# A hybrid decoder layer on one core: two of the four weight-block sums of the seven-product down projection are made in DRAM by accumulating DMAs

## The chip, the cores and the metric

The kernel runs on 1 core of one Trainium2 chip. The metric is the device time in microseconds (us) of one execution. Five engines work beside each other and meet at semaphores: TensorE (PE in the profile), VectorE (DVE), ScalarE (ACT), GpSimd (POOL) and SyncE (SP). Sixteen DMA engines move the data that SP, ACT and POOL ask for.

## The reference

One layer of a hybrid decoder on 512 tokens and 16 learned meta tokens, model width 2048, all in float32, cut to what matters here:

```
p = rms_norm(h_res) @ w_in                        # 2048 columns in, conv and RWKV heads out
y_conv = short_conv_group(p[:, conv columns])     # width 3, gated
y_rwkv = rwkv7_group(token_shift(p[:, rest]))     # a recurrence over the tokens, 16 heads of 64
h_res += concatenate(y_conv, y_rwkv) @ w_out
h = rms_norm(h_res)
h_res += square(relu(h @ w_up)) @ w_down          # w_up 2048 x 8192, w_down 8192 x 2048
out = rms_norm(h_res)[16:]
```

## The kernel before

**Weights.** Every weight comes in quarters of 128 x 512 float32 (256 KB, in runs of 512 bytes) into a raw buffer. ScalarE rounds it to the upper part (w_hi), VectorE makes the rest (w_lo = raw - w_hi, split_mlp and split), and TensorE multiplies three times (hi by hi, hi by lo, lo by hi). w_hi and w_lo are rings of 8 quarters. SP asks for each quarter as soon as the one that lay in its raw buffer has been split. There are 4 raw buffers (w_raw) until the MLP and 8 in it (w_more as well).

**The recurrence stage.** It goes over 8 pairs of heads, some 91 us each. TensorE's instructions of a pair are one list: 96 steps of the next projection, and between them, at places that the table PACE fixes, the small matmuls of the recurrence (names such as gram0, x16, y0, z2). TensorE takes the list in order, and so do the others. In the middle of a pair the 64 x 64 triangular blocks (NA) are inverted, and their parts are laid out anew by way of DRAM. SP does this in exchange(): at i = 15 NA goes to DRAM (`gram<-NA`, L555), and 80 blocks of 16 x 16 come back onto 80 partitions (`UU<-gram`, L557, 1280 runs of 64 bytes). VectorE inverts them (from L1526 to L1531). At i = 17 they go out (`inverse<-UU`, L561), and at i = 18 they come back as rows (`uni<-inverse`, L564 and L565, and from ACT's queue L1068 and L1069). The step x16 on TensorE (L2001) needs them.

**GpSimd in a pair.** pair() on POOL makes rb_lo (L770) and the two masked copies of NA (nm16 and nm32, L775, four instructions) as soon as VectorE has written NA. Then it issues the DMAs that store the pair's results (L800, L785) and load the next pair's small weights.

**The MLP.** w_up's 8192 columns are taken in 8 groups of 1024. In each of the first 7 groups up() makes 8 tiles of 128 (512 columns of tokens in one matmul), and down() multiplies the group's 1024 rows of w_down by them in a seven-product form (Strassen-Winograd: 2 x 2 blocks of the weights and of the activations, 7 products of half size in place of 8). It takes 8 steps p, each with the products p1, p5, p2, p6, p4, p3, p7 of one tile, 84 matmuls of 256 columns. The last group is taken plainly.

Four of the seven products take a sum of weight blocks, with signs as the form needs them. sum_blocks() makes them on VectorE in three instructions for each p: two sums at once out of a21 and out of a11 and a22 (L1327, 128 x 1024), then a sum with a11 (L1331) and then one with a12 (L1335), both 128 x 512. split_mlp(i) on VectorE calls it before and behind w_lo of p1 and behind w_lo of p5. Splits run 8 quarters ahead of TensorE, so in the last up tile (t = 7) the quarter split is p1 of p = 1, and its sums stand there too, between scale() (L1684, which takes the up tile out of PSUM) and the forms of the activations (L1708 to L1693) that down() waits for.

**The results of down()** are added to the residual in DRAM: one accumulating DMA of 512 KB for each p, issued by POOL (L844, `residual<-delta`).

Of the kernel before, what the change touches and what calls it, by code (L numbers as in the profile page):

```python
# [31 lines left out]
P = 128  # L32
# [81 lines left out]
def at(static, per=0, it=0):  # L114

    return it * per + static
# [95 lines left out]
SUM_STEP = {"p5": 1, "p7": 1, "p6": 2, "p3": 3}  # L212
# [5 lines left out]
L_GROUP = 4 * UT + 4 * HALF_KT  # L218
R_LAST = Q_MLP + R_GROUP * (FFG - 1)
L_LAST = L_GROUP * (FFG - 1)  # L220
T_LAST = T_MLP + UT * FFG
# [10 lines left out]
def hybrid_layer(nc, x, meta, norm_mix_g, w_in, shift_mu, conv_w, decay_w0, decay_w2, iclr_a0, iclr_a2,  # L232
# [4 lines left out]

    res_dram = nc.dram_tensor("residual", [D, SEQ], F32, kind="Internal").ap()
    y_dram = nc.dram_tensor("mixed", [D, SEQ], F32, kind="Internal").ap()
    gram_dram = nc.dram_tensor("gram", [2 * SLOTS * 2, CHUNK], F32, kind="Internal").ap()  # L240
    inv_dram = nc.dram_tensor("inverse", [2 * 2 * SLOTS * 2, CHUNK], F32, kind="Internal").ap()
    as_rows = lambda ap: ap[:, 0:C * C].rearrange("(x a) (r c) -> a r x c", a=2, c=C)
# [127 lines left out]
    w_sum = sb("w_sum", [P, 4, KQ, P], on=post)  # L370
# [55 lines left out]
    sum_made, part_kept, combined = sem("sum_made"), sem("part_kept"), sem("combined")  # L426
    delta_added = [sem("delta_added0"), sem("delta_added1")]
    delta_taken = sem("delta_taken")
    res_back = sem("res_back")
    gained, fin_turned, fin_kept = sem("gained"), sem("fin_turned"), sem("fin_kept")  # L430
    rows_scaled = [sem("rows_scaled_dve"), sem("rows_scaled_act")]
# [52 lines left out]

        return (w_raw if rel % RAW_MLP < RAW else w_more)[:, rel % RAW]

    def raw_pair(p):

        return w_raw if p % 2 == 0 else w_more

    def bank_for(product, p):

        if product in ("p1", "p6", "p7"):
# [16 lines left out]
    wout_q = w_out.rearrange("(a k p) (m n) -> a p k m n", k=KQ, p=P, n=P)  # L510
    wup_q = w_up.rearrange("(a k p) (g m n) -> a p k g m n", k=KQ, p=P, g=FFG, n=P)
    wdn_q = w_down.rearrange("(g a k p) (m n) -> g a p k m n", g=FFG, k=KQ, p=P, n=P)

    RS_CUT = META + 3 * P

# [4 lines left out]
    def _(sp):  # L520
# [83 lines left out]
        def freed_by(rel):  # L604

            shift, i = divmod(rel, L_GROUP)
            if i < R_UP:
                return Q_MLP + R_GROUP * shift + i + 1
            p, b = divmod(i - R_UP, 4)
            return Q_MLP + R_GROUP * shift + R_UP + NP * p + (2, 2, 5, 3)[b]  # L610

        for rel in range(RAW_MLP):
            load_mlp(wup_q[rel % 4, :, :, 0, ORDER[rel // 4], :], rel, Q_MLP - RAW + rel + 1 if rel < RAW else None)
        with sp.Fori(0, FFG - 1) as g:
            for t in range(RAW_MLP // 4, UT):
                for a in range(4):
                    rel = 4 * t + a
                    load_mlp(wup_q[a, :, :, g, ORDER[t], :], rel, freed_by(rel - RAW_MLP), g)
            for p in range(HALF_KT):
                for b, name in enumerate(BLOCKS):  # L620
                    rel = R_UP + 4 * p + b
                    load_mlp(wdn_q[g, int(name[2]) - 1, :, :, p + HALF_KT * (int(name[1]) - 1), :], rel, freed_by(rel - RAW_MLP), g)
# [26 lines left out]
    def _(pool):  # L649
# [99 lines left out]
        def load_g(j):  # L749
            pool.dma_start(g_w[:], gate_g2[0:P, bass.ts(j, P)]).then_inc(g_loaded, 16)  # L750
            for first in range(0, TAIL, GATE_TAIL):
                pool.dma_start(g_w2[first:first + GATE_TAIL, :], gate_g2[P:P + GATE_TAIL, bass.ts(j, P)]).then_inc(g_loaded, 16)

        def pair(j, last=False):
            n = [0]

            def done(name, ins):
                assert POOL_STEPS[n[0]] == name
                n[0] += 1
                ins.then_inc(pool_done, 1)  # L760

            if not last:
                pool.wait_ge(pe_done, step(PE_STEPS, "low", j))
                load_wa(j + 1)

            if last:
                pool.wait_ge(z_done, at(6, 3, j))
                load_y(0, 1)
            pool.wait_ge(act_done, step(ACT_STEPS, "rbh", j))
            done("rbl", nc.gpsimd.tensor_tensor(rb_lo, ld[:, 0:SEQ], rb_hi.bitcast(F32), ALU.subtract))  # L770
            pool.wait_ge(dve_done, step(DVE_STEPS, "gram0", j))
            for i, m in enumerate(LEVELS):
                mask = level_mask[:, i, :].unsqueeze(1).to_broadcast([P, SLOTS, C])
                for h in range(2):
                    ins = nc.gpsimd.tensor_tensor(NM[m][:, h, :, :], NA[:, h, :, 0, :], mask, ALU.mult)  # L775
                done(f"nm{m}", ins)
            if last:
                load_y(2, 3, 4, 5)
            store_conv(j)
            if last:  # L780
                load_y(*range(6, KT - 1))
            else:
                split_squares(j + 1)
                pool.wait_ge(dve_done, step(DVE_STEPS, "y4", j))
                pool.dma_start(y_view[:, bass.ds(j + PAIRS, 1), :], bt[:, PAD + META:TP].unsqueeze(1)).then_inc(y_stored, 16)  # L785
                load_g(j + 1)
# [82 lines left out]
    def _(act):  # L869
# [35 lines left out]
        def split_mlp(i, it=0):  # L905

            shift, j = divmod(i, R_GROUP)
            product = PRODUCTS[(j - R_UP) % NP] if j >= R_UP else None
            if product in SUM_IN:
                act.wait_ge(sum_made, at(3 * ((j - R_UP) // NP) + SUM_STEP[product], 3 * HALF_KT, it))  # L910
                src = w_sum[:, SUM_IN[product]]
            else:
                rel = L_GROUP * shift + (j if product is None else R_UP + 4 * ((j - R_UP) // NP) + BLOCKS.index(BLOCK_IN[product]))
# [343 lines left out]
    def _(dve):  # L1257
# [41 lines left out]
        def split_mlp(i, it=0):  # L1299
# [4 lines left out]
            if product == "p1":  # L1304
                sum_blocks(p, 0, it)
            rel = L_GROUP * shift + (j if product is None else R_UP + 4 * p + BLOCKS.index(BLOCK_IN.get(product, "a11")))
            src = w_sum[:, SUM_IN[product]] if product in SUM_IN else raw_mlp(rel)
            dve.wait_ge(hi_split, at(Q_MLP + i + 1, R_GROUP, it))
            r = (Q_MLP + i) % RING
            V.tensor_tensor(w_lo[:, r], src, w_hi[:, r].bitcast(F32), ALU.subtract).then_inc(lo_split, 1)  # L1310
            if product in ("p1", "p5"):
                sum_blocks(p, 1 if product == "p1" else 2, it)

        def sum_blocks(p, which, it):

            raw = raw_pair(p)

            def loaded(name):
                rel = R_UP + 4 * p + BLOCKS.index(name)
                dve.wait_ge(raw_loaded[rel % RAW_MLP], at(raw_sum(rel), 16 * L_GROUP // RAW_MLP, it))  # L1320

            if which == 0:
                for name in ("a11", "a21", "a22"):
                    loaded(name)
                dve.wait_ge(lo_split, at(Q_MLP + R_UP + NP * p, R_GROUP, it))
                flat = lambda ap: ap.rearrange("p s k n -> p s (k n)")
                V.tensor_tensor(flat(w_sum[:, 0:2]), flat(raw[:, 1:2]).to_broadcast([P, 2, KQ * P]), flat(raw[:, 0:3:2]),  # L1327
                                ALU.add).then_inc(sum_made, 1)
            if which == 1:
                dve.wait_ge(sum_made, at(3 * p + 1, 3 * HALF_KT, it))  # L1330
                V.tensor_tensor(w_sum[:, 2], raw[:, 0], w_sum[:, 1], ALU.add).then_inc(sum_made, 1)  # L1331
            if which == 2:
                loaded("a12")
                dve.wait_ge(sum_made, at(3 * p + 2, 3 * HALF_KT, it))
                V.tensor_tensor(w_sum[:, 3], raw[:, 3], w_sum[:, 2], ALU.add).then_inc(sum_made, 1)  # L1335

        def split_last(i):

# [916 lines left out]
```

## Time and profile before

| | |
|---|---|
| time before, median of 3 runs | 2351.0 us (2350.06 to 2352.89) |
| the profiled execution | 2349.79 us, its span 2348.1 us |
| TensorE busy | 2320.8 us, 99% |
| VectorE busy | 1491.3 us, 64% |
| ScalarE busy | 1019.9 us, 43% |
| GpSimd busy | 299.7 us, 13% |
| DMA | 286.18 MB, 122 GB/s on average |
| chain that ended last | TensorE 91% of the span |

A busy TensorE is the union of its overlapping matmuls, so what lies between 2320.8 and 2348.1 us is all that it stood still. The trace gives the start and the length of every instruction. For a DMA it gives the time from its issue to its landing.

### The profile page before, as it was taken

The numbers are of one execution on the slowest core, as the hardware profiler recorded it, in microseconds if no ns is written. First come the engines' busy times: TensorE is split into PE (matmuls) and PEld (weight loads), VectorE is DVE, ScalarE is ACT, GpSimd is POOL, SyncE is SP. The second block draws the span as 40 slices with busy tenths as digits, with TensorE's granted clock in tenths as the row PEclk, the third lists the DMA queues.
The fourth block names the chain that finished last, engine by engine and source line by source line (L and its number), as shares of the span: only waits on it lengthen the run. The fifth ranks groups of instructions, "written<-read, shape, count | busy, mean of one in ns | idle before, by whom it ended". The sixth has DMA issues, their size and how long they took to land.

```text
span 2348.1 us, 49773 instructions
## 1 busy us (share of the span) xinstructions
PE 2320.8 (99%) x18736; PEld 2087.0 (89%) x18736; DVE 1491.3 (64%) x2338; ACT 1019.9 (43%) x1808; POOL 299.7 (13%) x340
## 2 busy tenths in 40 slices
PE   8999999999999999999999999999999999999998
PEld 8999999999999788889889889889889899899888
DVE  7558668568567654548558468467467476475356
ACT  6534434434344322435435345345345344354336
POOL 5102011011012132101001001001001001001007
PEclk9999999999999999999999999999999999999999
DMA  8244243343343643526527527537447347347434
GB/s 253 72 108 101 68 112 80 93 103 75 98 103 100 181 130 98 179 86 144 145 72 160 138 81 162 131 94 168 110 98 177 99 101 175 94 117 195 120 110 142
DMA packets 513298, 286.18 MB, mean 122 GB/s; under 512 B 84510, under 2 KB 490528, under 8 KB 512672
## 3 DMA queue, kind: packets, MB, share of 16 engines
q1 hardware_dynamic: 478512, 224.19, 34.6%
q0 software_dynamic: 24064, 56.20, 11.8%
q10 hardware_dynamic: 10496, 2.62, 0.6%
q8 instruction: 161, 2.64, 0.5%
q14 instruction: 65, 0.53, 0.1%
HBM read 232.47 MB, written 50.47 MB: 121 GB/s over the span
## 4 chain that ended last, share of the span: by engine, by line
PE 91%; DVE 3%; DMA 3%; issue 1%; ACT 1%; SPq 0%; ACTq 0%; DVEq 0%
PE PD L1894 42%; PE PD L1899 18%; PE PW L2167 5%; PE PW L2168 5%; PE PW L2169 5%; PE PD L2167 2%; PE PD L2168 2%; PE PD L2169 2%; PE PD L2113 1%; PE PD L1923 1%; PE PW L1923 1%; DMA w_raw<-in_w_in 1%; PE PW L1973 1%; DMA gram<-NA 1%; PE PW L2073 1%
## 5 line engine op out<-in xcount | busy, mean ns | idle before, releaser
L1894 PE MATMUL PD<-act_lo,w_hi 128*128 128x512 f32 x1344 | 531.6, 396 | 0.0
L1894 PE MATMUL PD<-act_hi,w_hi 128*128 128x512 f32 x1344 | 529.5, 394 | 0.5 <-issue 0.5
L1894 PE MATMUL PD<-act_hi,w_lo 128*128 128x512 f32 x1344 | 528.5, 393 | 0.0
L2167 PE MATMUL PW<-form_hi,w_hi 128*128 128x256 f32 x1120 | 313.4, 280 | 0.0
L2169 PE MATMUL PW<-form_hi,w_lo 128*128 128x256 f32 x1120 | 312.6, 279 | 0.0
L2168 PE MATMUL PW<-form_lo,w_hi 128*128 128x256 f32 x1120 | 312.6, 279 | 0.0
L1894 PEld LDWEIGHTS PD<-act_hi,w_hi 128*128 128x128 f32 x1344 | 252.4, 188 | 62.7 <-issue 2.0
L1894 PEld LDWEIGHTS PD<-act_hi,w_lo 128*128 128x128 f32 x1344 | 252.9, 188 | 57.5
L1894 PEld LDWEIGHTS PD<-act_lo,w_hi 128*128 128x128 f32 x1344 | 252.1, 188 | 57.8 <-issue 0.2
L1345 DVE TENSOR_TENSOR w_lo<-w_raw,w_hi 128x512 fp32r<-128x512 f32 x268 | 206.7, 794 | 109.0 <-ACT w_hi L930 105.7
L930 ACT CAST w_hi<-w_raw 128x512 fp32r<-128x512 f32 x268 | 160.4, 620 | 252.2 <-DMA w_raw<-in_w_in 113.6
L1899 PE MATMUL PD<-act_hi,w_hi 128*128 128x264 f32 (+1 forms) x1248 | 264.9, 293 | 0.0
L1899 PE MATMUL PD<-act_hi,w_lo 128*128 128x264 f32 (+1 forms) x1248 | 251.3, 283 | 0.0
L1899 PE MATMUL PD<-act_lo,w_hi 128*128 128x264 f32 (+1 forms) x1248 | 251.2, 282 | 0.0
L1310 DVE TENSOR_TENSOR w_lo<-w_raw,w_hi 128x512 fp32r<-128x512 f32 x200 | 137.1, 689 | 125.5 <-ACT w_hi L917 102.6
L2167 PEld LDWEIGHTS PW<-form_hi,w_hi 128*128 128x128 f32 x1120 | 210.5, 188 | 1.7 <-issue 1.4
L1310 DVE TENSOR_TENSOR w_lo<-w_more,w_hi 128x512 fp32r<-128x512 f32 x200 | 137.4, 689 | 116.1 <-ACT w_hi L917 115.4
L2168 PEld LDWEIGHTS PW<-form_lo,w_hi 128*128 128x128 f32 x1120 | 210.5, 188 | 0.3
L2169 PEld LDWEIGHTS PW<-form_hi,w_lo 128*128 128x128 f32 x1120 | 210.5, 188 | 0.0
L844 POOL DMA_DIRECT2D residual<-delta x56 | 66.9, 1195 | 1115.5 <-DVE delta L1732 997.3
L1899 PEld LDWEIGHTS PD<-act_hi,w_hi 128*128 128x128 f32 x1248 | 192.5, 188 | 11.9 <-issue 6.7
L917 ACT CAST w_hi<-w_raw 128x512 fp32r<-128x512 f32 x200 | 123.2, 618 | 180.0 <-PE PD L1894 155.3
(378 smaller groups left out, 4080.7 us busy)
## 6 DMA issues: line engine op xcount, KB each, us to landing
w_raw<-in_w_in SPq DMA_DIRECT2D x200, 256.0 KB, 3.2
w_raw<-in_w_down SPq DMA_DIRECT2D x136, 256.0 KB, 3.0
w_more<-in_w_down SPq DMA_DIRECT2D x136, 256.0 KB, 3.1
w_raw<-in_w_up SPq DMA_DIRECT2D x128, 256.0 KB, 3.1
w_more<-in_w_up SPq DMA_DIRECT2D x128, 256.0 KB, 3.4
residual<-delta POOLq DMA_DIRECT2D x56, 512.0 KB, 5.8
w_raw<-in_w_out SPq DMA_DIRECT2D x64, 256.0 KB, 2.8
residual<-res POOLq DMA_DIRECT2D x4, 2048.0 KB, 10.1
```

The source lines that it names most:

```text
L844: pool.dma_start(res_view[:, p::HALF_KT, :], delta[:, p % 2].rearrange("p (a h) n -> p a (h n)", a=2), accum_op=ALU.add).then_inc(delta_ad ...
L917: nc.scalar.copy(w_hi[:, (Q_MLP + i) % RING], src).then_inc(hi_split, 1)
L930: nc.scalar.copy(w_hi[:, q % RING], w_raw[:, q % RAW]).then_inc(hi_split, 1)
L1310: V.tensor_tensor(w_lo[:, r], src, w_hi[:, r].bitcast(F32), ALU.subtract).then_inc(lo_split, 1)
L1345: V.tensor_tensor(w_lo[:, q % RING], w_raw[:, q % RAW], w_hi[:, q % RING].bitcast(F32), ALU.subtract).then_inc(lo_split, 1)
L1894: ins = M(pd_seq(n)[:, 0:width], w, v[:, k, first:first + width], start=begin, stop=end)
L1899: ins = M(PD[:, 2 * (n % 2) + a, cols], w, v[:, k, start:start + cols.stop - cols.start], start=begin, stop=end)
L1923: ins = M(bank[:, h, cols], w, v[:, k, start:start + cols.stop - cols.start], start=begin, stop=end)
L1973: ins = M(PW[rows_of(c), 2 * h + k // 4, k % 4 * P:(k % 4 + 1) * P], (bt if name == "gram0" else kt)[hs[h], cols], ar[hs[h], :, cols], sta ...
L2167: M(bank_for(product, p), whi, hi, start=begins and k == 0, stop=False, skip_group_check=True)
L2168: M(bank_for(product, p), whi, lo, start=False, stop=False, skip_group_check=True)
L2169: ins = M(bank_for(product, p), wlo, hi, start=False, stop=ends and k == KQ - 1, skip_group_check=True)
```

## The change

Two of the four sums are no longer made on VectorE: s1 = a21 + a22 (p5) and s3 = a11 + a21 (p7). For each group and each sum a DMA now copies the 512 x 1024 block a21 (2 MB, rows of 4 KB) from w_down to a DRAM tensor (copy_block), and a second, accumulating one adds the other block to it (add_block), which waits until the copy has landed. s1 and s3 are then loaded as a fourth and a fifth raw quarter of each p (before: a11, a21, a22, a12; now: a11, s1, a12, a22, s3). VectorE still makes the other two sums, of 128 x 512 each: a11 + s1, and a12 with that.

The sums of groups 0 to 3 are made in the recurrence stage, one for each pair: pair j adds its sum and copies the block of the next. The sums of groups 4 to 6 are made in the MLP, at the head of GpSimd's loop body for groups 0 to 2. All of these DMAs are issued by POOL.

```diff
-BLOCKS = ("a11", "a21", "a22", "a12")
-BLOCK_IN = {"p1": "a11", "p2": "a12", "p4": "a22"}
-SUM_IN = {"p5": 1, "p6": 2, "p3": 3, "p7": 0}
+BLOCKS = ("a11", "s1", "a12", "a22", "s3")
+BLOCK_IN = {"p1": "a11", "p5": "s1", "p2": "a12", "p4": "a22", "p7": "s3"}
+FREED_BY = (3, 3, 4, 5, 7)
+SUM_IN = {"p6": 0, "p3": 1}
+SUMMED_IN_MIX = 4
...
             for p in range(HALF_KT):
                 for b, name in enumerate(BLOCKS):
+                    if name[0] == "s":
+                        if p == 0:
+                            sp.wait_ge(block_summed, at(32, 32, g))
+                            sp.sem_inc(sum_seen, 1)
+                        src = sums_q[name == "s3"][g, :, :, p, :]
...
+        def copy_block(g, column):
+            dst = s3_dram if column else s1_dram
+            pool.dma_start(dst[g], wdn_halves[g, 1, 0]).then_inc(block_copied[column], 16)
+
+        def add_block(g, column, copies, per=0, it=0):
+            pool.wait_ge(block_copied[column], at(16 * copies, 16 * per, it))
+            pool.sem_inc(copy_seen, 1)
+            dst = s3_dram if column else s1_dram
+            pool.dma_start(dst[g], wdn_halves[g, 1 - column, 1 - column], accum_op=ALU.add).then_inc(block_summed, 16)
...
                 done(f"nm{m}", ins)
+            add_block(j // 2, j % 2, j // 2 + 1)
+            if j + 1 < 2 * SUMMED_IN_MIX:
+                copy_block((j + 1) // 2, (j + 1) % 2)
             if last:
                 load_y(2, 3, 4, 5)
             store_conv(j)
...
         split_squares(0)
+        copy_block(0, 0)
         for j in range(PAIRS - 1):
             pair(j)
...
-        with pool.Fori(0, FFG - 1) as g:
+        with pool.Fori(0, FFG - 1 - SUMMED_IN_MIX) as g:
+            copy_block(g + SUMMED_IN_MIX, 0)
+            copy_block(g + SUMMED_IN_MIX, 1)
+            add_block(g + SUMMED_IN_MIX, 0, SUMMED_IN_MIX + 1, 1, g)
+            add_block(g + SUMMED_IN_MIX, 1, SUMMED_IN_MIX + 1, 1, g)
+            add_deltas(g)
+        with pool.Fori(FFG - 1 - SUMMED_IN_MIX, FFG - 1) as g:
+            add_deltas(g)
...
-            if product in ("p1", "p5"):
-                sum_blocks(p, 1 if product == "p1" else 2, it)
+            if product in ("p5", "p2"):
+                sum_blocks(p, 0 if product == "p5" else 1, it)
```

Two places show what moves. The first is GpSimd's order in one pair of the recurrence stage (the second of the 8). Before (L770 is rb_lo, L775 the four masked copies, `mixed` the store of the results):

```order
L770 TENSOR_TENSOR rb_lo<-uni,rb_hi 128x512
L775 TENSOR_TENSOR uni<-NA,level_mask 128x320 x4
L800 DMA mixed<-cx 128x512
L747 TENSOR_TENSOR k_sq_lo<-uni,k_sq_hi 128x528
L785 DMA mixed<-bt 128x512
```

and with the change (the line numbers are those of the changed kernel):

```order
L793 TENSOR_TENSOR rb_lo<-uni,rb_hi 128x512
L798 TENSOR_TENSOR uni<-NA,level_mask 128x320 x4
L775 DMA first_column_sum<-in_w_down 512x1024
L768 DMA second_row_sum<-in_w_down 512x1024
L826 DMA mixed<-cx 128x512
L758 TENSOR_TENSOR k_sq_lo<-uni,k_sq_hi 128x528
L811 DMA mixed<-bt 128x512
```

Two DMAs of 2 MB, the accumulating one first, now stand right behind the masked copies of NA and ahead of the pair's stores.

The second place is VectorE at the last up tile of a group (`form<-PD` is scale(), `form<-form` and `form_lo` are the forms that down() waits for). Before:

```order
L1684 SCALAR_TENSOR_TENSOR form<-PD,rs 128x512
L1320 REGISTER_ALU
L1327 TENSOR_TENSOR w_sum<-w_more 128x1024
L1308 REGISTER_ALU
L1310 TENSOR_TENSOR w_lo<-w_more,w_hi 128x512
L1330 REGISTER_ALU
L1331 TENSOR_TENSOR w_sum<-w_more,w_sum 128x512
L1703 REGISTER_ALU
L1708 SCALAR_TENSOR_TENSOR form<-form 128x256
```

and with the change, behind the same scale() and the same forms:

```order
L1717 TENSOR_TENSOR form_lo<-form,form_hi 128x768
L1343 REGISTER_ALU
L1345 TENSOR_TENSOR w_lo<-w_more,w_hi 128x512
L1355 TENSOR_TENSOR w_sum<-w_more 128x512
L1343 REGISTER_ALU
L1345 TENSOR_TENSOR w_lo<-w_more,w_hi 128x512
L1358 REGISTER_ALU
L1359 TENSOR_TENSOR w_sum<-w_more,w_sum 128x512
```

The sums have moved from ahead of the forms to behind them, and the one of 128 x 1024 is gone.

## Rows read from the trace of the kernel before

**Rows 1.** The page, part 1: busy time, share of the span, instructions

```profile
PE 2320.8 (99%) x18736; PEld 2087.0 (89%) x18736; DVE 1491.3 (64%) x2338; ACT 1019.9 (43%) x1808; POOL 299.7 (13%) x340
```

**Rows 2.** Waits of TensorE, 1000 to 2150 us: total, times, longest

```profile
PE PD L2167 <- DVE form_lo L1693: 6.1, 7, 0.9
```

**Rows 3.** Up, then down: us; busy of PE, PEld, DVE, ACT, POOL; clock; DMA share; GB/s

```profile
1136.00:1225.00 89.00, 89.00 (x387) 72.19 (x386) 41.94 (x67) 30.86 (x49) 1.20 (x1) 1.00 0.36 100
1225.00:1304.00 79.00, 78.11 (x666) 77.67 (x665) 64.86 (x105) 45.60 (x91) 8.35 (x7) 1.00 0.68 153
```

**Rows 4.** Timeline of VectorE behind an up stage: start, length, instruction

```profile
1225.32 0.69 DVE L1684 SCALAR_TENSOR_TENSOR form<-PD,rs 128x512 f32<-128x512 f32 x1 [1.43 <-PE PD L1894]
1225.93 1.22 DVE L1327 TENSOR_TENSOR w_sum<-w_more 128x1024 f32<-128x1024 f32 x1
...
1228.27 0.42 DVE L1708 SCALAR_TENSOR_TENSOR form<-form 128x256 f32<-128x256 f32 x1
...
1229.27 0.68 DVE L1693 TENSOR_TENSOR form_lo<-form,form_hi 128x512 fp32r<-128x512 f32 x1
```

**Rows 5.** Timeline of TensorE at the same place; idle before it in brackets

```profile
1230.01 0.38 PE L2167 MATMUL PD<-form_hi,w_hi 128*128 128x256 f32 x1 [0.88 <-DVE form_lo L1693]
```

**Rows 6.** Tile w_sum, one of two buffers: duration ns min/median/max, first and last

```profile
L1327 DVE TENSOR_TENSOR w_sum<-w_raw x28: 1215/1215/1220, 1038.5 to 2122.0; 128x1024 f32<-128x1024 f32 x28
L1331 DVE TENSOR_TENSOR w_sum<-w_raw,w_sum x28: 682/685/687, 1040.3 to 2123.8; 128x512 f32<-128x512 f32 x28
```

**Rows 7.** Timeline of SP's DMA queue in the third pair

```profile
303.48 0.34 SPq L557 DMA_DIRECT2D UU<-gram  x1
...
313.02 1.02 SPq L561 DMA_DIRECT2D inverse<-UU  x2
...
316.50 0.60 SPq L564 DMA_DIRECT2D uni<-inverse  x1
```

**Rows 8.** Timeline of GpSimd in the third pair

```profile
297.20 4.86 POOL L775 TENSOR_TENSOR uni<-NA,level_mask 128x320 f32<-128x320 f32 x4 [0.54 <-DVE NA L1474]
```

**Rows 9.** Timelines of VectorE and of TensorE in the third pair

```profile
306.33 0.07 DVE L1526 MEMSET UU<- 80x16 f32 x1 [1.60 <-DMA UU<-gram]
...
323.42 0.69 PE L2001 MATMUL PW<-uni 64*64 64x64 f32 x32
```

**Rows 10.** DMA issues, 295 to 345 us: KB each, us to landing

```profile
UU<-gram SPq DMA_DIRECT2D x1, 80.0 KB, 2.7
...
uni<-inverse SPq DMA_DIRECT2D x1, 80.0 KB, 5.6
```

**Rows 11.** Waits of TensorE, 180 to 750 us (six pairs)

```profile
PE PW L2001 <- DMA uni<-inverse: 0.4, 1, 0.4
```

**Rows 12.** DMA, 968 to 982 us: packets, MB, share; then issues

```profile
q0 software_dynamic: 994, 4.01, 77.3%
q1 hardware_dynamic: 918, 0.46, 12.2%
...
residual<-res POOLq DMA_DIRECT2D x2, 2048.0 KB, 11.3
w_more<-in_w_up SPq DMA_DIRECT2D x4, 256.0 KB, 11.1
```

**Rows 13.** DMA, 1068 to 1077 us, one accumulating DMA: packets, MB, share

```profile
q0 software_dynamic: 272, 0.52, 40.2%
```

**Rows 14.** The last pair: GpSimd's timeline, then the chain, and its DMA issues

```profile
756.22 1.11 POOL L796 DMA_DIRECT2D yin<-mixed  x2
...
757.64 4.57 DMA UU<-gram
...
yin<-mixed POOLq DMA_DIRECT2D x4, 256.0 KB, 4.0
```

**Rows 15.** Windows with two 2 MB DMAs under way, and behind the last matmul

```profile
968.00:982.00 14.00, 14.00 (x59) 10.72 (x58) 9.06 (x12) 5.93 (x11) 1.82 (x2) 1.00 0.90 319
...
2340.00:2348.00 8.00, 0.00 (x0) 0.00 (x0) 1.58 (x3) 2.31 (x3) 0.00 (x0) 0.53 0.66 262
```

More of the change, by code:

```diff
@@ L217 @@
 R_GROUP = R_UP + NP * HALF_KT
-L_GROUP = 4 * UT + 4 * HALF_KT
+L_GROUP = 4 * UT + NB * HALF_KT
 R_LAST = Q_MLP + R_GROUP * (FFG - 1)
@@ L239, in hybrid_layer @@
     y_dram = nc.dram_tensor("mixed", [D, SEQ], F32, kind="Internal").ap()
+    s1_dram = nc.dram_tensor("second_row_sum", [FFG, SEQ, DH], F32, kind="Internal").ap()
+    s3_dram = nc.dram_tensor("first_column_sum", [FFG, SEQ, DH], F32, kind="Internal").ap()
     gram_dram = nc.dram_tensor("gram", [2 * SLOTS * 2, CHUNK], F32, kind="Internal").ap()
@@ L428, in hybrid_layer @@
     delta_taken = sem("delta_taken")
+    block_copied = [sem("block_copied_s1"), sem("block_copied_s3")]
+    block_summed, copy_seen, sum_seen = sem("block_summed"), sem("copy_seen"), sem("sum_seen")
     res_back = sem("res_back")
@@ L512, in hybrid_layer @@
     wdn_q = w_down.rearrange("(g a k p) (m n) -> g a p k m n", g=FFG, k=KQ, p=P, n=P)
+    wdn_halves = w_down.rearrange("(g y r) (x n) -> g x y r n", g=FFG, y=2, x=2)
+    sums_q = [d.rearrange("g (k p) (m n) -> g p k m n", p=P, n=P) for d in (s1_dram, s3_dram)]
     RS_CUT = META + 3 * P
@@ L608, in freed_by @@
                 return Q_MLP + R_GROUP * shift + i + 1
[L609 to L610 removed]
+            p, b = divmod(i - R_UP, NB)
+            return Q_MLP + R_GROUP * shift + R_UP + NP * p + FREED_BY[b]
         for rel in range(RAW_MLP):
@@ L620, in _ @@
                 for b, name in enumerate(BLOCKS):
-                    rel = R_UP + 4 * p + b
-                    load_mlp(wdn_q[g, int(name[2]) - 1, :, :, p + HALF_KT * (int(name[1]) - 1), :], rel, freed_by(rel - RAW_MLP), g)
+                    rel = R_UP + NB * p + b
+                    if name[0] == "s":
[3 more added lines that the diff above has]
+                        src = sums_q[name == "s3"][g, :, :, p, :]
+                    else:
+                        src = wdn_q[g, int(name[2]) - 1, :, :, p + HALF_KT * (int(name[1]) - 1), :]
+                    load_mlp(src, rel, freed_by(rel - RAW_MLP), g)
             for t in range(RAW_MLP // 4):
@@ L909, in split_mlp @@
             if product in SUM_IN:
-                act.wait_ge(sum_made, at(3 * ((j - R_UP) // NP) + SUM_STEP[product], 3 * HALF_KT, it))
+                act.wait_ge(sum_made, at(2 * ((j - R_UP) // NP) + SUM_IN[product] + 1, 2 * HALF_KT, it))
                 src = w_sum[:, SUM_IN[product]]
             else:
-                rel = L_GROUP * shift + (j if product is None else R_UP + 4 * ((j - R_UP) // NP) + BLOCKS.index(BLOCK_IN[product]))
+                rel = L_GROUP * shift + (j if product is None else R_UP + NB * ((j - R_UP) // NP) + BLOCKS.index(BLOCK_IN[product]))
                 act.wait_ge(raw_loaded[rel % RAW_MLP], at(raw_sum(rel), 16 * L_GROUP // RAW_MLP, it))
@@ L1303, in split_mlp @@
             p = (j - R_UP) // NP
-            if product == "p1":
-                sum_blocks(p, 0, it)
-            rel = L_GROUP * shift + (j if product is None else R_UP + 4 * p + BLOCKS.index(BLOCK_IN.get(product, "a11")))
+            rel = L_GROUP * shift + (j if product is None else R_UP + NB * p + BLOCKS.index(BLOCK_IN.get(product, "a11")))
             src = w_sum[:, SUM_IN[product]] if product in SUM_IN else raw_mlp(rel)
@@ L1310, in split_mlp @@
             V.tensor_tensor(w_lo[:, r], src, w_hi[:, r].bitcast(F32), ALU.subtract).then_inc(lo_split, 1)
-            if product in ("p1", "p5"):
-                sum_blocks(p, 1 if product == "p1" else 2, it)
+            if product in ("p5", "p2"):
+                sum_blocks(p, 0 if product == "p5" else 1, it)
         def sum_blocks(p, which, it):
[L1316 to L1320, printed above, removed]
+            at_ = R_UP + NB * p
             if which == 0:
-                for name in ("a11", "a21", "a22"):
-                    loaded(name)
+                dve.wait_ge(hi_split, at(Q_MLP + R_UP + NP * p + 2, R_GROUP, it))
                 dve.wait_ge(lo_split, at(Q_MLP + R_UP + NP * p, R_GROUP, it))
[L1326 to L1335, printed above, removed]
+                V.tensor_tensor(w_sum[:, 0], raw_mlp(at_), raw_mlp(at_ + 1), ALU.add).then_inc(sum_made, 1)
+            else:
+                dve.wait_ge(hi_split, at(Q_MLP + R_UP + NP * p + 3, R_GROUP, it))
+                dve.wait_ge(sum_made, at(2 * p + 1, 2 * HALF_KT, it))
+                V.tensor_tensor(w_sum[:, 1], raw_mlp(at_ + 2), w_sum[:, 0], ALU.add).then_inc(sum_made, 1)
         def split_last(i):
```

7 lines of the change are left out of this document (3 added, 4 removed).

## The prediction

> **What bounds the kernel now.** I read the busy shares of the page first. TensorE works 2320.8 of 2348.1 us [rows 1], so everything that a change can give back by relieving another engine lies in the 27 us in which TensorE stands. VectorE's 1491 us are no bound by themselves.
>
> The waits of TensorE come next. In the whole MLP but its last group there is one kind that counts, 6.1 us in 7 waits of up to 0.9 us, for form_lo [rows 2]. That is once per group, at the turn from up to down. The windows of one group agree: 89.00 of 89 us busy in the up stage, 78.11 of 79 in the down stage [rows 3]. VectorE is busy for 64.9 of those 79 us, below its limit.
>
> Then the recurrence stage, where TensorE's list is gapless too: in six pairs it waits for the inverse's blocks once, for 0.4 us [rows 11]. That is a chain that is met just in time, not one that is short. I followed it in the third pair, on the timelines. The read back of NA is issued at 303.48 and lands 2.7 us later [rows 7, 10]. VectorE starts on it at 306.33 [rows 9]. The parts go out at 313.02, are asked back at 316.50, and the later of the two reads lands 5.6 us after its issue, at about 316.50 + 0.60 + 5.6 = 322.7 [rows 7, 10]. TensorE takes x16 at 323.42 [rows 9]. So this chain of three trips through DRAM has 0.7 us to spare. While VectorE waits for the read at L1526, its later splits and its copies out of PSUM stand behind it, so TensorE would first stop at a tile that needs a bank, and then at x16; the end of it is the same.
>
> **The change, part by part.**
>
> *VectorE, removed.* Per p the 1.215 us sum becomes one of 0.685 us (a11 + s1), the two others become one: 1.215 + 0.685 + 0.685 - 2 x 0.685 = 1.2 us less [rows 6], the third taken as long as the second. Over 56 p that is 68 us of VectorE. TensorE waits for VectorE in one place only, so most of it is worth nothing. The place is the turn: between scale() at 1225.32 and the first form at 1228.27 stand the sum of 1.22 us, one split, and the second sum [rows 4]. Both sums leave. The instructions overlap a little, so about 1.7 us go: form_lo would be ready that much before its end at 1229.95, where TensorE waited 0.88 us for it [rows 4, 5]. The wait goes entirely, **-6.1 us** in 7 groups. What would be late next is ScalarE's rounding of the same forms; it starts from the same instructions that move up, so I count on no new wait. Below, this gain is 0 if the wait only changes its name; it can't be above 6.1.
>
> *Loads in the down stage.* Five quarters per p in place of four: 8 x 256 KB = 2.1 MB more in 79 us. The queue's price at 512-byte runs is 12.2% of 14 us for 0.46 MB [rows 12], 3.7 us per MB, so 8 us more: the DMA share goes from 0.68 to about 0.78 [rows 3]. A raw buffer is freed at least 8 quarters, some 11 us, before its next content is split; even beside 4 MB of other traffic a load took 11.1 [rows 12]. Cost 0; the cover is the ring of 8 split quarters.
>
> *The sums of groups 4 to 6.* Each time 4 DMAs of 2 MB at the head of an up stage. Their price: 77.3% of 14 us moved 4.01 MB [rows 12], so 5.7 us for a copy of 2.1 MB. The accumulating DMA took 40.2% of 9 us for 0.52 MB [rows 13], 3.6 us; by its bytes that is 14.6 us for 2.1 MB, by its packets (272 against 528) 7.0 us. Together 25 to 41 us beside an up stage that uses 0.36 of the DMA engines for 89 us [rows 3]. Where 4 MB of such traffic ran before, four weight quarters took 11.1 us to land [rows 12], and TensorE was still busy for all 14 us [rows 15]: 16 quarters lie ahead of it there. I take 0, with 5 us a group as the other end.
>
> *The sums of groups 0 to 3, in the recurrence stage.* This is the term that decides. POOL is done with the masked copies at 297.20 + 4.86 = 302.06 [rows 8] and issues the accumulating DMA there, then the copy; its wait for the copy before is long satisfied, and nothing else of its own is due soon behind them. The read `UU<-gram` is issued at 303.48, 1.4 us later, on the same 16 engines. What happens to it? Two places of the trace tell.
> - In the last pair two reads of 256 KB each are issued by POOL at 756.22, again 1.4 us before the read back of NA at 757.64, which then takes 4.57 us in place of 2.7 [rows 14, 10]. At 2.7 us per MB the two are 1.4 us of work: the read waited for all of it, and a bit.
> - Beside the two 2 MB stores, the queue of the weights got 0.46 MB through against 4.01 MB, in 918 packets against 994 [rows 12]. It went packet by packet, so a queue of small packets loses by their size. The read back of NA is in 1280 packets of 64 bytes; the add and the copy together are 1024 of 4 KB. Turn by turn, it would be done no earlier than both of them.
>
> So behind the add alone the read lands 14.6 us late, and with the copy 14.6 + 5.7 = 20.3. Less 0.7 us to spare, 13.9 and 19.6 us a pair. The copy is issued only when the add's descriptors are written, about when the read arrives, so I take **15 us** in each of 7 pairs, and 14 in the last, which has no copy: 7 x 15 + 14 = **+119 us**. At the low end the add costs 7.0 us by its packets and is alone ahead: 8 x 6.3 = +50. At the high end both are ahead at full price: 7 x 19.6 + 14 = +151. TensorE takes its list in order, so no matmul fills the hole.
>
> The Trainium skill, "DMA: Bandwidth & Descriptors", section "Queues, rings and completion order", says that each DMA engine goes round its queues packet by packet. The 918 against 994 packets agree. By this rule taken strictly, the sum would be the high end, +151 - 6 = +145 us, in place of +113.
>
> *TensorE's clock.* It is granted 1.00, the 2.4 GHz level, in every working window. Behind the last matmul it stood still, and 8 us of that are at 0.53, which is 1.2 GHz for nearly all of it [rows 15]. Holes of 14 us may bring this down, and the first matmuls behind each may run at half speed. No row shows how it rises again; I put 0 in the sum and 2 us a pair, +16, at the high end.
> The Trainium skill, "TensorE: Matmul & The Clock Gate", Part 1, says that an idle window drops the clock to half and some microseconds of work restore it; by it some 2 us a pair would be added, an estimate.
>
> **Sum.** -6.1 + 119 = +113 us on the profiled execution's 2349.8 us: 2463. The median of the runs is 1.2 us above that execution: **2464 us**.
>
> **The rivals.**
> - *The DRAM traffic is hidden.* The engines are half idle in the recurrence stage, and if small reads overtook the large packets nothing would be late: 2351 - 6 = **2345 us**, faster by 0.26%. For it: no wait of TensorE came from the stores of rows 12. Against it: those had 16 quarters of cover, this chain has 0.7 us. It decides at a delay of under 0.8 us a pair (6.1 / 8).
> - *The first read escapes, the second trip is caught.* If the add's first packets come after the 303.48 read, it lands on time. The parts' way out at 313.02 [rows 7] then waits for the end of add and copy, near 303.5 + 1 + 20.3 = 325, in place of landing by 316.5: 8.5 us, less 0.7. 7 x 7.8 = 55, little in the last pair, less 6: **2400 us**.
> - *Dearer still.* Both ends of these DMAs are in DRAM, which no row shows. If that doubles the add, or the up stages of three groups run dry of weights, +190 us or more: **above 2540 us**.
>
> **How the numbers follow.** A measurement of this kernel can tell about 0.2%, 5 us. Chances: the forecast with its ends, 2397 to 2530, 0.59; the second trip caught (from 2375 to 2397 when the add is cheap), 0.20; hidden, 0.10; the loss within a microsecond a pair, so that gain and loss cancel, 0.04; dearer, 0.07. The range is 2375 to 2530: outside are hidden, cancelled and dearer. Low end: the second-trip case with the add at 7.0 us; high end: 151 + 16 + 15 - 6 = 176, 2527. Faster 0.10, same 0.04, slower 0.86.
>
> **What would show it.** In the changed kernel's waits: TensorE's row for form_lo gone, and new rows in the recurrence stage, at L2001's successor for the inverse or at the start of a tile for VectorE's copy out of PSUM, about 15 us a pair. SP's read of the 64-byte blocks should take 16 to 23 us to land in place of 2.7, the add some 15 and the copy 6 us more than their fixed part. VectorE's busy time falls by 68 us; each MLP group loses 0.9 us. If the read back of NA still lands in 3 us, the step that fails is the one on who waits at the DMA engines, and the time is one of the first two rivals'.

## The result, and the profile after

The change makes the kernel slower: 2507.6 us (median of 4 runs, 2497.9 to 2512.6) against 2350.5 us, ratio 1.066, interval 1.064 to 1.069. The forecast was 2464 us, in a range of 2375 to 2530. The profiled execution took 2497.9 us, its span is 2496.4 us.

The page of the kernel after: busy shares and instructions, then the chain that ended last by engine.

```profile
PE 2332.9 (93%) x18736; PEld 2098.3 (84%) x18736; DVE 1431.4 (57%) x2282; ACT 1013.5 (41%) x1808; POOL 324.4 (13%) x368
...
PE 81%; DMA 10%; DVE 6%; issue 1%; ACT 1%; SPq 0%; POOL 0%; ACTq 0%; DVEq 0%; POOLq 0%
```

VectorE lost 60 us of busy time, where 68 were foreseen. The lengths of its instructions, added up, fall by 70 us, but neighbours overlap a little, and busy time counts that once. TensorE now stands for 2496.4 - 2332.9 = 163.5 us, where it was 27 [rows 1], and it is busy for 12 us more with the same 18736 instructions. Its waits say where (total, times, longest):

```profile
PE PD L1923 <- DVE cu L1605: 118.7, 7, 17.1
PE PD L2137 <- DVE cu L1605: 12.1, 1, 12.1
PE PD L1918 <- DVE form L1708: 8.7, 1, 8.7
PE PD L1918 <- issue: 6.2, 3, 3.1
```

Seven waits of 17 us and one of 12 are the eight pairs of the recurrence stage. The row for form_lo [rows 2] is gone. The two others are in up stages of the MLP. VectorE's copy out of PSUM (`cu`, L1605) is named, but VectorE itself was held. Its own waits have this row:

```profile
DVE UU L1550 <- DMA UU<-gram: 160.4, 8, 20.9
```

In the third pair the chain in order of time (start, length) and the DMA issues of 335 to 400 us (KB each, us to landing) show the read back of NA. Before, it took 2.7 us [rows 10]:

```profile
341.62 21.41 DMA UU<-gram
```

```profile
second_row_sum<-in_w_down POOLq DMA_DIRECT2D x1, 2048.0 KB, 15.4
first_column_sum<-in_w_down POOLq DMA_DIRECT2D x1, 2048.0 KB, 22.1
...
inverse<-UU SPq DMA_DIRECT2D x2, 80.0 KB, 2.8
UU<-gram SPq DMA_DIRECT2D x1, 80.0 KB, 21.4
```

The read ends with the copy. The second trip, `inverse<-UU`, is as fast as it was, as the traffic is over by then.

GpSimd's timeline has the two DMAs where the order of instructions put them. The add is issued 1.6 us and the copy 0.9 us ahead of the read at 341.62, so both are there before it:

```profile
340.00 1.11 POOL L775 DMA_DIRECT2D second_row_sum<-in_w_down  x1
340.71 1.03 POOL L768 DMA_DIRECT2D first_column_sum<-in_w_down  x1
```

Windows of the same pair (length; busy of PE, PEld, DVE, ACT, POOL; granted clock; DMA share; GB/s):

```profile
355.00:360.00 5.00, 0.00 (x0) 0.00 (x0) 0.00 (x0) 0.00 (x0) 0.00 (x0) 0.75 0.99 309
360.00:365.00 5.00, 0.00 (x0) 0.00 (x0) 1.60 (x9) 1.08 (x2) 0.00 (x0) 0.50 0.40 115
...
370.00:372.00 2.00, 1.01 (x4) 1.01 (x5) 1.93 (x4) 0.00 (x0) 0.00 (x0) 0.50 0.64 63
372.00:374.00 2.00, 2.00 (x12) 2.00 (x11) 1.96 (x4) 0.00 (x0) 0.00 (x0) 0.50 0.73 150
374.00:376.00 2.00, 2.00 (x16) 2.00 (x16) 0.84 (x2) 0.57 (x1) 0.00 (x0) 0.86 0.52 120
376.00:378.00 2.00, 2.00 (x19) 2.00 (x18) 1.29 (x2) 0.05 (x1) 0.33 (x1) 1.00 1.33 241
```

While TensorE stands, its clock falls to 0.50, the 1.2 GHz level. It starts again at 371 us, still at that level, and 1.00 is back 3.6 us later (1.01 and 2.00 us of the windows above, and 0.56 us of the one at 0.86). Half of that is lost, some 1.8 us in this pair. In seven pairs that is about the 12 us of added busy time.

In the MLP, SP's timeline for group 0 shows the up stage running dry. Beside the two copies and the two adds, the issue alone of four weight quarters took 24 us:

```profile
1130.83 24.26 SPq L606 DMA_DIRECT2D w_more<-in_w_up  x4
1155.34 16.26 SPq L606 DMA_DIRECT2D w_raw<-in_w_up  x4
```

### The profile page after: what moved, and what is told of

It is laid out like the page before. It is cut to its first block, busy times and chain, and to the rows that moved or that the text cites. A ratio compares the mean times of both kernels' runs of the same rounds, so it can differ in the third digit from the quotient of the medians.

```text
span 2496.4 us, 49726 instructions
## 1 busy us (share of the span) xinstructions
PE 2332.9 (93%) x18736; PEld 2098.3 (84%) x18736; DVE 1431.4 (57%) x2282; ACT 1013.5 (41%) x1808; POOL 324.4 (13%) x368
## 4 chain that ended last, share of the span: by engine, by line
PE 81%; DMA 10%; DVE 6%; issue 1%; ACT 1%; SPq 0%; POOL 0%; ACTq 0%; DVEq 0%; POOLq 0%
PE PD L1918 35%; PE PD L1923 15%; DMA UU<-gram 7%; PE PW L2192 5%; PE PW L2193 5%; PE PW L2191 5%; PE PD L2192 2%; PE PD L2193 2%; PE PD L2191 2%; DMA w_more<-in_w_up 2%; PE PD L2137 1%; DMA gram<-NA 1%; DVE w_lo L1369 1%; PE PD L1947 1%; PE PW L1947 1%
## 5 line engine op out<-in xcount | busy, mean ns | idle before, releaser
L1923 PE MATMUL PD<-act_hi,w_hi 128*128 128x264 f32 (+1 forms) x1248 | 270.7, 299 | 118.7 <-DVE cu L1605 118.7
L967 ACT CAST w_hi<-w_raw 128x512 fp32r<-128x512 f32 x268 | 161.4, 620 | 394.3 <-DMA w_raw<-in_w_in 228.8
L1345 DVE TENSOR_TENSOR w_lo<-w_raw,w_hi 128x512 fp32r<-128x512 f32 x256 | 175.1, 689 | 181.0 <-ACT w_hi L954 141.1
L1345 DVE TENSOR_TENSOR w_lo<-w_more,w_hi 128x512 fp32r<-128x512 f32 x256 | 175.7, 690 | 166.2 <-ACT w_hi L954 160.9
L1369 DVE TENSOR_TENSOR w_lo<-w_raw,w_hi 128x512 fp32r<-128x512 f32 x268 | 207.2, 796 | 106.8 <-ACT w_hi L967 103.7
L954 ACT CAST w_hi<-w_raw 128x512 fp32r<-128x512 f32 x256 | 157.1, 617 | 217.5 <-PE PD L1918 142.2
L954 ACT CAST w_hi<-w_more 128x512 fp32r<-128x512 f32 x256 | 157.1, 618 | 204.7 <-PE PD L1918 147.4
```

The costliest lines, as they stand in the source:

```text
L967: nc.scalar.copy(w_hi[:, q % RING], w_raw[:, q % RAW]).then_inc(hi_split, 1)
L1369: V.tensor_tensor(w_lo[:, q % RING], w_raw[:, q % RAW], w_hi[:, q % RING].bitcast(F32), ALU.subtract).then_inc(lo_split, 1)
L1923: ins = M(PD[:, 2 * (n % 2) + a, cols], w, v[:, k, start:start + cols.stop - cols.start], start=begin, stop=end)
```

## The experiments

**Each part alone.** First the VectorE side without any DRAM traffic. In the changed kernel the calls of copy_block and add_block are left out, with SP's wait for the sums, and the two added quarters come from another block of w_down, so the down product's results are those of wrong blocks.

```diff
-                        src = sums_q[name == "s3"][g, :, :, p, :]
+                        src = wdn_q[g, 0, :, :, p + HALF_KT, :]
...
-            add_block(j // 2, j % 2, j // 2 + 1)
-            if j + 1 < 2 * SUMMED_IN_MIX:
-                copy_block((j + 1) // 2, (j + 1) % 2)
```

> The changed kernel without its sums in DRAM: no copying and no accumulating DMA is issued, and in place of s1 and s3 SP loads the block a21 straight from w_down, five quarters per p as in the changed kernel; the results of the down product are those of wrong blocks. What stays is the VectorE side of the change and the fifth load. Theory A (all of the loss comes from the DMAs that POOL issues, and the wait for form_lo at the turn from up to down is gone with the sums that stood ahead of it): 2350.5 - 6 = 2344 to 2345 us, and no row for form_lo among TensorE's waits. Theory B (the fifth load or the new order of VectorE costs something itself): above 2350 us, with a new wait of TensorE in the down stages.

Measured: 2339.6 us, ratio 0.995 (0.994 to 0.997), 11.3 us faster. A holds in its mechanism, with nearly twice the size; there is no row for form_lo among TensorE's waits.

The kernel before with the recurrence stage's traffic alone (its results unused):

```diff
                 done(f"nm{m}", ins)
+            add_block(j // 2, j % 2, j // 2 + 1)
+            if j + 1 < 2 * SUMMED_IN_MIX:
+                copy_block((j + 1) // 2, (j + 1) % 2)
```

> The kernel before, with the copying and accumulating DMAs of the recurrence stage added (the first copy and one add and one copy behind the masked blocks in each pair, all as in the changed kernel) and their results unused; VectorE makes its four sums as before. Theory A (the loss is the read of the 16 x 16 blocks that stands behind this traffic): 17 us of standing per pair and 2 us for the lower clock behind it, 7 x 19 + 14 = 147 us, so 2498 us, with the read landing after 21 us. Theory B (the recurrence stage and the MLP share the loss, as the fifth load and the traffic of the MLP cost too): under 2460 us.

Measured: 2494.3 us, 1.061 (1.060 to 1.063), +143.4 us against the kernel before in the same runs (2350.9). A holds. Its waits are those of the changed kernel, with the old row for form_lo back:

```profile
PE PD L1922 <- DVE cu L1604: 118.5, 7, 17.4
PE PD L2136 <- DVE cu L1604: 12.2, 1, 12.2
PE PD L2190 <- DVE form_lo L1716: 6.1, 7, 0.9
```

And with the traffic of the MLP alone:

```diff
+        with pool.Fori(0, FFG - 1 - SUMMED_IN_MIX) as g:
+            copy_block(g + SUMMED_IN_MIX, 0)
+            copy_block(g + SUMMED_IN_MIX, 1)
+            add_block(g + SUMMED_IN_MIX, 0, 1, 1, g)
+            add_block(g + SUMMED_IN_MIX, 1, 1, 1, g)
+            add_deltas(g)
```

> The kernel before, with only the six sums of the MLP added (two copies and two accumulating DMAs at the head of GpSimd's loop body for groups 0 to 2), results unused. Theory A (the up stages run dry of weights for a few us, as the trace of the changed kernel shows 8.7 and 6 us of waits in its first two groups): 2350.5 + 15 = 2362 to 2370 us. Theory B, that of the prediction (hidden by the 16 quarters that lie ahead of TensorE): within 1 us of the kernel before.

Measured: 2369.5 us, 1.008 (1.006 to 1.010), +18.6 us. A holds, and the zero of the prediction falls. 15 of the 18.6 us are in new waits of TensorE:

```profile
PE PD L1923 <- issue: 7.6, 2, 4.2
PE PD L1923 <- DVE form L1713: 7.3, 1, 7.3
```

The three parts add up to -11.3 + 143.4 + 18.6 = +150.7, against +157.1 for the whole.

**The gain without the change.** In the kernel before, only VectorE's order at the last up tile is changed:

```diff
                 scale(t)
-                split_mlp(e + RING, g)
+                if t < UT - 1:
+                    split_mlp(e + RING, g)
                 dve.wait_ge(u_sq, at(t + 1, UT, g))
...
                     low(t, 4, 7, 3)
+                if t == UT - 1:
+                    split_mlp(e + RING, g)
```

> The kernel before, with nothing moved to DRAM: at the last up tile of a group VectorE makes the forms of the activations first, and then the split and the sums of weight blocks that stood ahead of them. Theory A (what the change gains is only that these 1.7 us leave that place): the same gain as with VectorE's sums taken away, 2344 to 2345 us. Theory B (the gain, where there is one, needs VectorE's lower load): no change, or slower as the splits of the first products come 2 us later.

Measured: 2340.3 us, 0.996 (0.994 to 0.997), 10.6 us faster, the same as the VectorE side of the change (2339.6). The 60 us of VectorE's work were worth nothing beyond the place of two sums. Why 10.6 and not 6.1? TensorE's timeline of before, the matmul ahead of the wait that [rows 5] shows:

```profile
1228.86 0.28 PE L2169 MATMUL PD<-form_hi,w_lo 128*128 128x256 f32 x1
```

The next one starts at 1230.01, 1.15 us later, where 0.12 is usual in this stretch: 1.03 us are lost, and the wait counts 0.88, since a matmul's modelled end lies behind the next one's start. The matmuls right behind the wait come late as well. The sixth of them is this one:

```profile
1230.97 0.28 PE L2169 MATMUL PW<-form_hi,w_lo 128*128 128x256 f32 x1
```

The five steps to it took 0.96 us in place of 0.59. Why they did, the trace does not show; with the new order both losses are gone. Together they are 1.4 us. The up tile that the chain names behind each down stage gives the period of a group, before and then with the new order:

```profile
1643.42 11.15 PE PD L1894 x48
1812.50 11.15 PE PD L1894 x48
```

```profile
1637.82 11.15 PE PD L1897 x48
1805.53 11.15 PE PD L1897 x48
```

169.1 and 167.7 us, the same 1.4 us a group; from the first group to the last the two traces part by 9.3 us.

**Who waits at the DMA engines.** Three variants of the traffic beside the read. First, the changed kernel with the read in 80 runs of 1 KB:

```diff
-sp.dma_start(UU[0:NBLK, 0, :].rearrange("b (s t) -> b s t", t=BASE), gram_blocks[:, 0])
+sp.dma_start(UU[0:NBLK, 0, :], gram_dram[0:2 * SLOTS * 2, 0:C // BASE * BASE * BASE].rearrange("m (b e) -> m b e", e=BASE * BASE))
```

> The changed kernel, where the read back of NA onto 80 partitions takes the same 80 KB as 80 runs of 1 KB in place of 1280 of 64 bytes (other elements than it needs, so the layer's result is wrong). Theory A (the DMA engines go round the queues packet by packet: the read has 80 packets on each engine against 32 of the add and 32 of the copy, so it can't end before both; with 5 packets on each it needs 5 turns): it lands within 3 to 6 us. The second trip, issued some 10 us after the read's issue, is then the one that is caught until the traffic ends 20 us after that issue: about 8 us of standing per pair in place of 17, and 2440 us in all. Theory B (first come, first served: the read stands behind all that was queued before it, whatever its packets are): it still takes some 20 us to land, and the time stays near 2500 us.

Measured: 2462.0 us, 1.047. The chain of its third pair:

```profile
330.30 9.29 DMA UU<-gram
...
346.59 10.21 DMA inverse<-UU
```

B falls: the same 80 KB, issued at the same place, land in 9.3 us in place of 21.4. The second trip is now the one caught, as A said. A's number (2440) was too low. TensorE stands for 10 us a pair in place of 8 (35.4 us in seven waits for the inverse's blocks and 35.1 in seven for `cu`), and there are now two holes in each pair, with the granted clock at 0.50 behind both:

```profile
348.00:351.00 3.00, 3.00 (x16) 3.00 (x15) 2.76 (x5) 0.29 (x1) 0.00 (x0) 0.50 0.86 206
363.50:368.00 4.50, 4.46 (x64) 4.14 (x68) 1.99 (x3) 1.24 (x2) 0.00 (x0) 0.50 0.94 258
```

TensorE's busy time is 2355.3 us, 22 us more than in the changed kernel, whose standing is longer but in one piece.

Why the read took 9.3 us and not 3 to 6, the packets say. First DMA queues of this run from the read's issue at 330.3 to 334.9 us (q0 is POOL's queue, q1 SP's; packets, MB, share), then the changed kernel's from 346.6 to 351.6 and from 351.6 to 356.6:

```profile
q0 software_dynamic: 156, 0.64, 93.2%
```

```profile
q0 software_dynamic: 244, 1.00, 103.0%
q1 hardware_dynamic: 242, 0.02, 7.6%
...
q0 software_dynamic: 374, 1.47, 96.5%
q1 hardware_dynamic: 375, 0.02, 7.1%
```

Once the read has its turn, packet goes for packet: 242 beside 244, 375 beside 374, whether they hold 64 bytes or 4 KB. Ahead of that, no packet of SP's queue is moved for 4.6 us, while 156 of POOL's are, 10 for each engine. That the engines had taken these already is a guess; the trace does not show where they stood.

Second, the changed kernel with the copy issued at the end of the pair:

```diff
-            if j + 1 < 2 * SUMMED_IN_MIX:
-                copy_block((j + 1) // 2, (j + 1) % 2)
...
                 load_g(j + 1)
+                copy_block((j + 1) // 2, (j + 1) % 2)
```

> The changed kernel, where only the accumulating DMA stays behind the masked blocks and the copy of the next block is issued at the end of the pair, behind its last store and small loads. Theory A (turn by turn, the read has to wait for each of the 4 KB packets that are there, 32 per engine of the add at 0.33 us and 32 of the copy at 0.2 us): the read lands 12 to 13 us after its issue in place of 21, the standing falls from 17 to 8 or 9 us a pair, and the time to about 2507 - 7 x 8.5 = 2447 us. Theory B (the add alone is what it waited for, the copy runs behind the read): no change, near 2505 us.

Measured: 2454.4 us, 1.045, 53 us less than the changed kernel; A (2447) holds, B falls. The read landed after 14.5 us, and the seven waits fell from 118.7 to 67.8 us:

```profile
PE PD L1922 <- DVE cu L1604: 67.8, 7, 10.0
PE PD L2136 <- DVE cu L1604: 12.1, 1, 12.1
```

The read waited for the copy too, although that is issued behind the add. The last pair, which never had a copy, is unchanged.

Third, half of the traffic: dram_sums_beside_recurrence with `[0:256]` behind both operands of its copies and adds.

> dram_sums_beside_recurrence (2494.3 us) with the first 256 of the 512 rows in each of its copies and adds: half the traffic, at the same places. Theory A (the read of the 16 x 16 blocks, with 80 packets per engine, outlasts the 16 and 16 packets of add and copy too, so the standing is the length of the traffic less what the chain has to spare): the read lands after 11 to 12 us, 8 us of standing a pair and 1 to 2 us of low clock, 2350.5 + 7 x 9 + 5 = 2419 us. Theory B (a fixed cost of a large transfer beside the read): above 2460 us.

Measured: 2422.8 us, 1.031, against 2419 expected. DMA issues of 320 to 330 us, and TensorE's waits:

```profile
UU<-gram SPq DMA_DIRECT2D x1, 80.0 KB, 12.9
```

```profile
PE PD L1922 <- DVE cu L1604: 51.9, 7, 8.3
PE PD L2136 <- DVE cu L1604: 7.0, 1, 7.0
```

Half the bytes, half the loss (72 of 143 us): the large fixed cost of B is not there.

**Other places for the traffic.** Add and copy behind the store of the convolution's result, when the inverse is back:

```diff
             store_conv(j)
+            add_block(j // 2, j % 2, j // 2 + 1)
+            if j + 1 < 2 * SUMMED_IN_MIX:
+                copy_block((j + 1) // 2, (j + 1) % 2)
```

> The changed kernel, with the add and the copy of each pair issued behind the store of the convolution's result, when the inverse's blocks are back, in place of ahead of the read. Theory A (the loss is the place: nothing small and urgent runs in the 20 us behind this point, only weight quarters): the read lands in 3 us again, and what stays is the up stages' 19 us less the 11 us gained on VectorE, plus up to 5 us a pair if the weight quarters, at one packet in turn with one of 4 KB, come late: 2360 to 2395 us. Theory B (any 20 us of such traffic in a pair costs about as much, as the weights then come late): above 2440 us.

Measured: 2399.0 us, 1.021 (1.019 to 1.023). The read lands in 2.5 us again. But 2399 - 2350.5 - 18.6 + 11.3 = 41 us are still lost in the recurrence stage, above what A allowed (2395) and far below B. The waits are spread over many steps now, most of them for ScalarE or with no releaser shown:

```profile
PE PW L2061 <- ACT uni L1110: 12.1, 1, 12.1
PE PW L2093 <- issue: 8.1, 6, 2.4
```

In the third pair the four weight quarters issued beside add and copy took 17.2 us to land (median), and ScalarE, which rounds them in order, comes late to its steps of the recurrence. The longest wait, 12.1 us, has another cause. It is in the last pair, where the chain runs over a load of stored results that POOL issued behind the add:

```profile
802.51 17.27 DMA yin<-mixed
```

So part of what is lost is again a small, urgent load behind large packets.

The same, with the MLP's six sums one to a group, in groups 0 to 5:

```diff
+        for i in range(2 * (FFG - 1 - SUMMED_IN_MIX)):
+            n, column = SUMMED_IN_MIX + i // 2, i % 2
+            copy_block(n, column)
+            add_block(n, column, n + 1)
+            add_deltas(i)
+        add_deltas(FFG - 2)
```

> As sums_behind_the_inverse, and the six sums of the MLP are made one per group in groups 0 to 5, in place of two per group in groups 0 to 2: a copy and an add of 2 MB at the head of each up stage. Theory A (16 quarters of cover in the up stage hold for 17 us of such traffic, not for 34): the 19 us of the MLP go, so 15 to 20 us less than sums_behind_the_inverse. Theory B (the same bytes cost the same wherever they are): the same time as sums_behind_the_inverse.

Measured: 2394.1 us (2386.9 to 2402.3), against 2399.0 (2392.2 to 2400.2): no difference that these runs can tell. In the MLP the run before had three waits, 14.3 us together. Now there are five small ones, and one more of 3.9 us:

```profile
PE PD L1916 <- DVE w_lo L1343: 12.5, 5, 3.4
```

So A fails here. Half as much at a time runs the up stage dry twice as often: one copy and one add are already too much in a row.

**Small pieces.** Each DMA of 2 MB is cut into four of 512 KB, issued one at a time (but for the first copy and the sum of the last pair), none near the inverse's trips. In the MLP one sum is made per group, in groups 0 to 5:

```diff
+                for n_, name in enumerate(("pq", "gh", "y0", "z3", "z5", "z7", "y", "var")):
+                    pool.wait_ge(pe_done, step(PE_STEPS, name, j))
+                    pool.sem_inc(copy_seen, 1)
+                    if n_ % 2 == 0:
+                        add_piece(j // 2, j % 2, n_ // 2)
+                    else:
+                        copy_piece((j + 1) // 2, (j + 1) % 2, n_ // 2)
...
+            for t in range(8):
+                pool.wait_ge(quarter_used, Q_MLP + R_GROUP * i + 4 * (t + 1) - 3)
+                pool.sem_inc(copy_seen, 1)
+                (copy_piece if t < 4 else add_piece)(n, column, t % 4)
```

> The changed kernel, all of its sums made, but in pieces of 512 KB that POOL issues one at a time: in each pair of the recurrence stage four pieces of the add and four of the next copy, each behind one of TensorE's steps pq, gh, y0, z3, z5, z7, y and var (none near the three trips of the inverse), the last sum in the stage of the output projection, and in the MLP one sum per group, one piece at each up tile. Theory A (what costs is only that 16 to 34 us of large packets stand together, ahead of something that is due sooner; the bytes alone cost nothing): as with no traffic at all, 2339.6 us measured, so 2338 to 2345 us. Theory B (the bytes cost wherever they are, as the pair of experiments behind the inverse suggests): 2370 us or more.

Measured over 11 runs: 2348.7 us, 1.000 (0.999 to 1.001): the same bytes, and the time of the kernel before. That is 9 us above the 2339.6 us that A named, and A's range ended at 2345; it is far below B's 2370. The windows of this kernel, the recurrence stage (to 830 us) and the MLP's first seven groups, then its waits for weights:

```profile
0.00:830.00 830.00, 818.44 (x9710) 760.46 (x9711) 568.07 (x895) 361.24 (x599) 182.98 (x258) 1.00 0.60 148
...
1000.00:2150.00 1150.00, 1142.90 (x7264) 1028.94 (x7263) 683.83 (x1128) 523.06 (x965) 96.72 (x100) 1.00 0.67 159
```

```profile
PE PD L1932 <- DVE w_lo L1359: 4.8, 3, 1.8
PE PD L1932 <- issue: 2.3, 2, 1.4
```

In the recurrence stage TensorE stands for 11.6 us, and it did for 11.9 before the change (818.15 busy us in the same window): there the traffic costs nothing now. In the MLP 7.1 us of waits for weights remain, some 7 of the 9 us.

## Why the prediction was right where it was, and what it mis-sized

**The mechanism held.** "This is the term that decides" was the add and the copy ahead of the read of the 16 x 16 blocks. The read is what VectorE waited for, the standing is in the place foreseen, and taking the traffic alone (+143), its copy away, its half, or another place for it each moved the time as a wait at the DMA engines would. The point of the forecast was less good than its range: it lies 44 us below the measured time, because the recurrence term and the MLP's were both too small, and the range is 155 us wide.

**The term of +119 us was 24 too small.** Two choices in it. "I take 15 us in each of 7 pairs", between the add alone ahead (13.9) and both (19.6): the standing was 17.0 us, and the run without the copy shows that the read waits for both. The reason given for 15 was that the copy is issued "about when the read arrives". It was issued 0.9 us ahead of it, and by the prediction's own count of turns it would have mattered little: 1280 small packets outlast the 1024 large ones. In the last pair 12.1 us stood against 14. The second choice was the clock, 0 in the sum and 16 us at the high end. The standing is 130.8 us by the waits; the rest of the 143 is the clock, some 1.6 us a pair.

**The prices.** The sentence on turns ("it would be done no earlier than both of them") was right: the read landed with the copy. The add's price of 14.6 us by its bytes was somewhat high, and the 7.0 by its packets far too low: with the add alone ahead the read landed 11.8 us later than before (14.5 against 2.7). Add and copy together took 20.3 us in the sum, and the read landed 18.7 us later. By the Trainium skill ("DMA: Bandwidth & Descriptors", "Queues, rings and completion order"), read strictly, the recurrence stage was to cost +151 us and the whole change +145. Without the clock, which was no part of these sums, the measured stage cost 130.8 us, and with it 143. The packet counts agree with the rule one for one. What the rule doesn't tell is the 4.6 us ahead of the first turn.

**The MLP's traffic was not free.** "I take 0, with 5 us a group as the other end": it cost 18.6 us, 6 in each of three groups. The step that failed is the comparison with 4 MB beside the up stage, where TensorE stayed busy. Here it was 8 MB in a row, with SP's issues held up as well (24 us for four), and that is more than the cover of 16 quarters. The bytes are not all of it: in the run with one sum per group 4 MB, a copy and then an add, ran the up stage dry too. The 4 MB of the comparison were two stores, which landed in 11.3 us [rows 12].

**The gain at the turn was 10.6, not 6.1 us.** "It can't be above 6.1" took the wait rows for the whole loss. From start to start of the matmuls 1.03 us are lost where 0.88 is shown, and 0.37 more behind the wait; the period of a group falls by 1.4 us. That the rest of VectorE's relief is worth nothing held: 2339.6 with it, 2340.3 without.

**Together** the terms were -6.1, +119, 0 for the MLP and 0 for the clock. Measured one by one: -11.3, +143.4 (the clock in it) and +18.6. The sum, +150.7, is 6 us short of the median's +157.1. The changed kernel's four runs lie 15 us apart, and the profiled one, the fastest of them, is 148.1 us above the profiled execution before. So the 6 us are in the three runs that have no trace, and their cause stays open.

**The low end of the range does not follow from its numbers.** 2375 us was to be the second trip caught "with the add at 7.0 us". By the prediction's own numbers the traffic then ends near 303.5 + 1 + 12.7 = 317.2 us, 0.7 us behind the 316.5 at which the parts land anyway. That is no more than the chain has to spare, and the time would be 2345 us. The bound played no part in the outcome.

**The better version** is the kernel before with the forms ahead of the sums: 2340.3 us against 2350.9 in the same runs, with no DRAM sums at all. Since the VectorE side with its traffic left out reaches 2339.6, making the sums in DRAM could win no more here that these runs can tell.

## What to carry to other kernels

Before work is moved to "idle" DMA engines, look at what is issued just behind it: a transfer of many small packets goes one for one with packets of 4 KB, and if it has more packets than they are, it ends when they end, however few bytes it has. Break such background traffic into pieces and place them by the progress of the engine that is the bound, away from any round trip that is met just in time. And before an engine is relieved of work, find the one place where the bound engine waits for it: moving a split and two sums past that place was worth as much as taking 60 us of work away.

## What the runs showed of the hardware that was not expected

- A queue that started while another one's large packets were under way got its first packets late, and only then its turns: 10 packets of 4 KB per engine, 4.6 us, went ahead of a read of 5 packets per engine, which took 9.3 us.
- SP is held as well. Issuing four loads took it 24 us beside two copies and two adds, against 8.4 us beside 4 MB of stores (at 972.84 us of the kernel before).
- The Trainium skill, "TensorE: Matmul & The Clock Gate", Part 1, has the clock fall when TensorE stands and rise again with work. Here it was at 0.50 from about 358 to 375 us of the changed kernel, of which TensorE worked in the last 3.6; at the turns of the kernel before, with waits of 0.9 us, it never left 1.00. Two holes a pair, with 10 us of standing, cost more of it than one of 17: TensorE was busy for 2355.3 us with them, and for 2332.9 in the changed kernel.
- The row of a wait can understate what the wait costs: 0.88 us shown, 1.03 lost from start to start, and 1.4 with the slower matmuls right behind it.
